# The NSA compression product in four column groups of TensorE, folded by a second matmul

## What is computed

```python
def compress_blocks(z, pe, w1, w2):
    B, S, d = z.shape
    r = CMP_LEN // CMP_STRIDE
    n = S // CMP_STRIDE
    ch = z.reshape(B, n, CMP_STRIDE, d)
    blocks = jnp.concatenate([ch[:, j:n - r + 1 + j] for j in range(r)], axis=2)
    nc = blocks.shape[1]
    blocks = (blocks + pe).reshape(B, nc, CMP_LEN * d)
    return jax.nn.gelu(blocks @ w1) @ w2
```

## Time and profile before

| | us |
|---|---|
| median of 3 runs | 1615.89 |
| lowest and highest | 1615.51, 1617.13 |
| the profiled execution | 1616.83 |
| its span | 1615.0 |
| TensorE busy in it | 1540.0 |
| VectorE busy in it | 1125.7 |
| ScalarE busy in it | 955.0 |

### The profile page before, as it was taken

How to read it: one execution, slowest core, us unless ns; L and a number is a source line. 1 busy time by engine, 2 the same in 40 slices (tenths; PEclk the granted TensorE clock), 3 DMA queues, 4 the chain that set the end, 5 groups by cost and what they waited for, 6 DMA issues and landing times.

```text
span 1615.0 us, 17783 instructions
## 1 busy us (share of the span) xinstructions
PE 1540.0 (95%) x7055; PEld 1232.4 (76%) x7055; DVE 1125.7 (70%) x967; ACT 955.0 (59%) x912; POOL 35.1 (2%) x73
## 2 busy tenths in 40 slices
PE   7999899999798979999999999999999999999996
PEld 5765688888685647788888888888888888888874
DVE  4513444544451437988888888888888888888895
ACT  5434434333332515777777777777777767777763
POOL 2000000000000000000000000000000000000010
PEclk9979999999998979999999999999999999999998
DMA  9520655554252046999989999999999999999992
GB/s 341 174 105 1 239 196 179 194 183 166 95 187 105 1 156 224 349 339 363 396 330 372 391 334 365 391 336 361 392 342 361 385 336 372 381 347 358 403 396 84
DMA packets 148629, 445.24 MB, mean 276 GB/s; under 512 B 9407, under 2 KB 21565, under 8 KB 148541
## 3 DMA queue, kind: packets, MB, share of 16 engines
q1 hardware_dynamic: 146836, 438.24, 73.8%
q0 software_dynamic: 1584, 5.77, 0.9%
q10 hardware_dynamic: 120, 0.04, 0.0%
HBM read 439.30 MB, written 4.72 MB: 275 GB/s over the span
## 4 chain that ended last, share of the span: by engine, by line
PE 89%; DVE 5%; ACT 3%; issue 1%; DMA 0%; POOL 0%; DVEq 0%; POOLq 0%; SPq 0%; ACTq 0%
PE bank L681 85%; PE bank L684 3%; DVE part_l L1494 3%; ACT part_h L1165 1%; ACT junk L1174 1%; ACT prob L1340 0%; DVE gm L1499 0%; DMA h<-in_x_dram 0%; DVE xs L1498 0%; ACT probT L1165 0%; DVE gg L1499 0%; DVE xT L1498 0%; POOL rs L643 0%; DVE y L1494 0%; DVE h L1494 0%
## 5 line engine op out<-in xcount | busy, mean ns | idle before, releaser
L1494 DVE TENSOR_TENSOR part_l<-ring,part_h 128x2048 fp32r<-128x2048 f32 x378 | 859.4, 2290 | 190.4 <-ACT part_h L1165 188.1
L1165 ACT ACTIVATE part_h<-ring 128x2048 fp32r<-128x2048 f32 x378 | 721.0, 1919 | 239.5 <-PE bank L681 239.2
L681 PE MATMUL bank<-part_h,xh 128*128 128x512 f32 x1120 | 447.4, 400 | 6.1 <-DVE part_l L1494 3.3
L681 PE MATMUL bank<-part_h,xl 128*128 128x512 f32 x1120 | 437.4, 391 | 0.0
L681 PE MATMUL bank<-part_l,xh 128*128 128x512 f32 x1120 | 436.3, 390 | 0.0
L681 PEld LDWEIGHTS bank<-part_h,xh 128*128 128x128 f32 x1120 | 210.4, 188 | 58.9 <-DVE part_l L1494 15.5
L681 PEld LDWEIGHTS bank<-part_h,xl 128*128 128x128 f32 x1120 | 210.2, 188 | 45.8
L681 PEld LDWEIGHTS bank<-part_l,xh 128*128 128x128 f32 x1120 | 210.7, 188 | 40.6
L681 PE MATMUL bank<-part_h,hTh 128*128 128x512 f32 x560 | 220.8, 394 | 3.6 <-DVE hTl L1494 2.6
L681 PE MATMUL bank<-part_h,hTl 128*128 128x512 f32 x560 | 218.4, 390 | 0.0
L681 PE MATMUL bank<-part_l,hTh 128*128 128x512 f32 x560 | 218.0, 389 | 0.0
(11 more groups left out here) (251 smaller groups left out, 985.7 us busy)
## 6 DMA issues: line engine op xcount, KB each, us to landing
ring<-in_moe_w_gate_dram SPq DMA_DIRECT2D x112, 1024.0 KB, 7.1
ring<-in_moe_w_up_dram SPq DMA_DIRECT2D x112, 1024.0 KB, 7.2
ring<-in_moe_w_down_dram SPq DMA_DIRECT2D x112, 1024.0 KB, 7.3
ring<-in_w_in_dram SPq DMA_DIRECT2D x7, 2048.0 KB, 7.9
ring<-in_dense_w_gate_dram SPq DMA_DIRECT2D x14, 1024.0 KB, 5.1
ring<-in_dense_w_up_dram SPq DMA_DIRECT2D x14, 1024.0 KB, 5.1
ring<-in_dense_w_down_dram SPq DMA_DIRECT2D x14, 1024.0 KB, 4.8
ring<-in_w_o_dram SPq DMA_DIRECT2D x4, 2048.0 KB, 7.8
```

Of the source, the lines that this page charges most:

```text
L681: return nc.tensor.matmul(o, lhsT, rhs, start=start, stop=stop)
L1165: return nc.scalar.activation(dst, src, ACT.Copy, scale=scale)
L1494: return nc.vector.tensor_tensor(o, a, b, op)
```

## The change

- `blk` gets 32 columns instead of 15; the 17 new ones are set to zero in every layer, behind the wait for `s_zp`, since the memory is used for other things between.
- The 16 matmuls of a product write 32 partitions each, at partition 32 (k mod 4) of `bank[1]`. Partition group c thus collects the steps k = c, c + 4, c + 8, c + 12, and each group opens with k < 4 and closes with k >= 12.
- ScalarE copies all 128 partitions of `bank[1]` to `conv_u`, without the Gelu.
- `fold` is a 128 x 16 matrix of zeros and ones, made once at the start from `ident`: row 32 c + r has its one in column r. The four transposes are replaced by four fp32 matmuls of `conv_u` with `fold`, which turn the values and add up the four groups.
- The Gelu then runs on ScalarE as it writes `hidT` and `hidR`, in three instructions; VectorE's three copies are gone.

```diff
@@ -144,6 +144,7 @@
         mv = sb("mv", [P, NB, 2])
+        fold = sb("fold", [P, 16])
         hidT = sb("hidT", [P, CH // P, 16])
@@ -219,7 +220,7 @@
-        blk = tsb("blk", [P, 2, 2, NC, 8])
+        blk = tsb("blk", [P, 2, 2, 32, 8])
@@ -814,8 +815,9 @@
                     for k in range(16):
-                        i = mm(bank[1][0:NC, j * CH:(j + 1) * CH], blk[:, j, k // 8, :, k % 8], w[:, k, :],
-                               k == 0, k == 15)
+                        c = 32 * (k % 4)
+                        i = mm(bank[1][c:c + 32, j * CH:(j + 1) * CH], blk[:, j, k // 8, :, k % 8], w[:, k, :],
+                               k < 4, k >= 12)
                     i.then_inc(s_hp, 1)
@@ -823,8 +825,8 @@
                 pe.wait_ge(s_hg, l + 1)
                 for j in range(2):
                     for t in range(CH // P):
-                        i = turn(bank[1][:, j * 32 + t * 16:j * 32 + t * 16 + NC],
-                                 conv_u[0:NC, j, t * P:(t + 1) * P], NC)
+                        i = mm(bank[1][:, j * 32 + t * 16:j * 32 + (t + 1) * 16],
+                               conv_u[:, j, t * P:(t + 1) * P], fold[:, :], True, True)
                 i.then_inc(s_hc, 1)
@@ -1314,8 +1316,15 @@
                 act.wait_ge(s_hp, 2 * l + 2)
-                nc.scalar.activation(conv_u[0:NC, :, :].rearrange("p b c -> p (b c)"), bank[1][0:NC, :],
-                                     ACT.Gelu_apprx_tanh).then_inc(s_hg, 1)
+                copy(conv_u[:, :, :].rearrange("p b c -> p (b c)"), bank[1][:, :]).then_inc(s_hg, 1)
+                act.wait_ge(s_hc, l + 1)
+                hid_ps = bank[1][:, 0:64].rearrange("p (j t c) -> p j t c", j=2, t=2)
+                nc.scalar.activation(hidT[:, :, 0:NC], hid_ps[:, 0, :, 0:NC], ACT.Gelu_apprx_tanh)
+                for t in range(CH // P):
+                    i = nc.scalar.activation(hidR[:, t, :, 0:NC],
+                                             hid_ps[:, 1, t:t + 1, 0:NC].to_broadcast([P, HEADS, NC]),
+                                             ACT.Gelu_apprx_tanh)
+                i.then_inc(s_hr, 1)
@@ -1499,6 +1508,8 @@
             dve.wait_ge(s_const, 1)
+            link(nc.vector.tensor_reduce(fold[:, :], ident[:, :].rearrange("p (c r) -> p r c", c=4)[:, 0:16, :],
+                                         AX_X, ALU.add))
@@ -1629,12 +1640,13 @@
                 dve.wait_ge(s_zp, l + 1)
+                nc.vector.memset(blk[:, :, :, NC:, :].rearrange("p j a c r -> p (j a) (c r)"), 0.0)
                 for j, name in enumerate(("pe_k", "pe_v")):
@@
-                        i = tt(blk[:, j, a, :, :], z[:, a:a + NC, :], pe_, ALU.add)
+                        i = tt(blk[:, j, a, 0:NC, :], z[:, a:a + NC, :], pe_, ALU.add)
@@ -1664,14 +1676,6 @@
-                dve.wait_ge(s_hc, l + 1)
-                hid_ps = bank[1][:, 0:64].rearrange("p (j t c) -> p j t c", j=2, t=2)
-                nc.vector.tensor_copy(hidT[:, :, 0:NC], hid_ps[:, 0, :, 0:NC])
-                for t in range(CH // P):
-                    i = nc.vector.tensor_copy(hidR[:, t, :, 0:NC],
-                                              hid_ps[:, 1, t:t + 1, 0:NC].to_broadcast([P, HEADS, NC]))
-                i.then_inc(s_hr, 1)
```

## The result

The changed kernel took 1598.6 us in the median of 4 runs (1597.33 to 1601.94), against 1615.74 for the kernel before on the same chip: a ratio of 0.9894, 95% interval 0.9882 to 0.9907, 17.1 us less. The forecast was 1601.7 with a range of 1598.0 to 1607.5. The profiled execution took 1597.33 us, 19.5 less than the profiled one of before; it is the fastest of the four, so the traces differ by 2.4 us more than the medians.

A forecast was written before the change was run, and what follows sets the result against it. TensorE, busy 95% of the span, was taken as the bound, with the compression products on the chain. Layer 0 -8.0 and layer 1 -6.2, together -14.2 us, took the median from 1615.89 to 1601.7, range 1598.0 to 1607.5.

The forecast's parts named there:

- The matmuls: Compression products: four column groups overlap by a factor of 4; first products -5.3 and -5.6 us, second 1.75 us warm.
- The second product is hidden: Second product fits under ScalarE's 4.1 us of copies and squares; only ScalarE's wait is gained, -3.0 us a layer.
- The table load: Ahead of the Gelu: the load runs beside the fold matmuls, -1.3 us in layer 0, none in layer 1.
- The fold: Four fp32 matmuls replacing the transposes: 1.8 and 1.7 us, so +1.4 and +1.3; bounds 1.0 and 1.8.
- Gelu after the fold: Three ScalarE instructions replace three VectorE ones between fold and w2: +0.15 us, bounds 0 and +0.4.
- The transposes: MLA transposes after the first product: 0.7 us still runs cold in layer 1, +0.35; no term in layer 0.
- What is free: Memset of blk's new columns, at most 0.7 us, and the one-time fold reduce delay nothing; SyncE's loads move forward.
- The clock outside the sum: Attention: the clock's rise may shift by 2.5 us, worth 1.2 us a layer either way, left out of the sum.
- no overlap: Rival: fp32 column groups in the products run one after another, total 1616 us; chance 0.06.
- slower: Rival: each change of column group drains the array, about 5 us more a product, total 1636 us; chance 0.04.
- Partial overlap: Rival: only two groups run at once in the products, giving back 3.4 us, total 1605.1; chance 0.16.
- The clock staying low: Rival: 1.2 GHz holds through transposes and second product, losing 2.0 and 1.4 us, total 1605.1; chance 0.12.

The follow-up runs named there:

- e_two_groups: The changed kernel with two column groups (partitions 0 and 64) instead of four: 1602.94 us against 1617.88 for the kernel before, ratio 0.9911.
- e_after_again: The changed kernel, unchanged, run and profiled once more: 1600.38 us against 1617.27 for the kernel before, ratio 0.9890.
- e_no_shift: The changed kernel with fold placed in an already free tile, so later tiles keep their old addresses: 1604.11 us against 1617.78 for the kernel before, ratio 0.9924.
- e_one_group: The changed kernel with all 16 matmuls of a product in the first 32 partitions: 1615.32 us against 1617.88 for the kernel before, ratio 0.9985.
- e_pad: The kernel before plus an unused SBUF tile of 64 bytes a partition where fold would lie: 1615.16 us against 1617.88 without it, ratio 0.9988.

## Why the prediction was right

**The matmuls.** The choice between a factor of 1 and 4 was the step with most in it. Warm, the second product went from 7.09 to 1.96 us, 3.6 times as fast, in which the last records still run for 0.2 us after the eight steps; at 1.2 GHz four records share 0.43. I had 1.75. The figure of the Trainium skill (TensorE: Matmul & The Clock Gate, Measured speedup vs the span model), 2.38 for three column tiles, would have made it an estimated 2.2 (7.09 / 3.2); this case measures less and sides with full overlap. The rule of the Trainium skill (TensorE: Matmul & The Clock Gate, The mechanism) that loads of weights overlap running matmuls only across row groups is contradicted by the trace after: four loads lie within 0.19 us, of which one alone lasts 0.14 or more, at the same rows and with matmuls in flight.

**The second product is hidden.** -3.0 in each layer came out as -3.1, and e_two_groups shows the cover: 3.68 us also fits under it. What I named as late next, ScalarE's copies and squares, was late next.

**The table load.** Hidden, as forecast: copy to copy 8.38 to 3.97 us in layer 0 is the wait of 3.02 and the load of 1.28. It came back by 0.2 where it outlasts the warm fold.

**The fold** was mis-sized in layer 0: 1.8 forecast, 1.07 measured, since the clock held. In layer 1 it took 1.89 for 1.7. In e_after_again layer 0 had 1.89 as well. The bounds 1.0 and 1.8 were right, the choice between them is the clock's. **Gelu after the fold**: I had +0.15; from the end of the fold to w2 it is 0.50 in layer 1, where 0.59 stood before, so nothing.

**The transposes.** 0.8 us too long in layer 0, where the clock rose 5.3 us after the start of the first product, not 2.9. I had carried the old distance over. The first product itself gained 4.9 for the 5.3. In layer 1 it rose 2.7 us after that start, not 4.1, so the product gained 5.8 for 5.6 and the +0.35 for cold transposes fell away. (I had also read the old fall of layer 0 as 103.9; the mean of 0.87 from 103 to 104 puts it at 103.7, which changes no term.)

**What is free.** The memset took 0.51 us and delayed nothing. But this part holds the one real omission: a tile of 64 bytes is not free or costly by what it holds; it moved in_h and in_l, and the projections gained 0.6 and 1.0 us in the trace after (1.7 and 0.8 between e_no_shift and the change on one chip). I put that term at nothing, and no row of before showed it.

**The clock outside the sum.** I left it out with 1.2 us a layer either way. It gave 2.0 us in gel/wsT, 0.5 in the attention of layer 1 and 1.0 ahead of the experts in the profiled execution; the median gained 2.4 less than that execution, and where isn't shown. The sum of -14.2 was right within 0.5 us for its own stretch, and part of that is luck: in layer 0 the late rise cost 0.4 in the product and 0.8 in the transposes, and the late fall gave 0.8 back in the fold. The median of 1598.6, 3.1 under the forecast, is the shift and the clock: e_no_shift, without the shift, gained 13.7. Two of its four executions lay below 1598.0, the low end of the range, so the range was placed too high by about the shift, and that the median still lies in it, by 0.6 us, is luck too.

The rivals: no overlap and slower are out (e_one_group is the first, and is what it looks like). Partial overlap exists, but by the order of the records and not by the hardware's number of groups. The clock staying low happened only in part, in layer 0's transposes.

## What to carry to other kernels

Small-output fp32 matmuls with a long sum can be spread over four column groups and folded by a small matmul; take turns between the groups matmul by matmul, since with four in a row to a group only two groups overlap. Count the gain only up to the next engine's work: here 3.1 of the second product's 5.1 us counted and the rest lay under ScalarE's work; moving its squares was worth another 4 us by the stages, and 7.5 in the total with the clock. Before crediting a few us to a change that adds a tile, run the old kernel with that tile unused.

## What the runs showed of the hardware

- Four column groups of fp32 matmuls at 256 columns run four at a time: 32 records in 1.96 us against 7.12 in one group, and 3.68 in two.
- Records overtake waiting ones of another group over a short reach only: with eight records in a row to a group, 4.72 us and never more than two groups.
- Moving SBUF tiles by 64 bytes changed the spacing of fp32r matmuls of 512 columns from 0.231 to 0.233 us to 0.227 in eleven traces out of eleven, and e_no_shift went back to 0.233. Why, which of the moved tiles it hangs on, and at which other shifts, was not tried.
- Executions of one program differ in where TensorE's clock rises and falls: at 87.3 and at 84.3 us for the same product of the same program, and in three traces of fourteen it fell for 3.4 us in the dense part, during or within 0.9 us after a standstill of TensorE of 2.59 us that all fourteen have. Ten runs of e_pad spread over 11 us, the faster with the higher mean granted clock.
- The same 16 records of gel/wsT took 3.65 us in the kernel before, where the clock had fallen at 79.8, ahead of them, and 1.98 us in e_pad, where it fell at 81.9, as they ended. In the kernel before it rose at 86.7, in the first product.
